# State-space output in the second block: rotated products added in pairs on GpSimd, two matrix terms per group on TensorE in place of four

## The chip, the core and the metric

The kernel runs on one core of a Trainium2 chip. The metric is the time of one execution on the device in microseconds (us), as a median over runs. The engines of the core are named here as in the profile: PE is TensorE (PEld its weight load), DVE is VectorE, ACT is ScalarE, POOL is GpSimd, and SP only issues transfers.

## What is computed

The program is two transformer-like blocks in a row, for 256 tokens of width 2048, in fp32. Each block projects, mixes (attention in the first; a matrix memory and a state-space layer in the second), and ends in an expert layer. The change is in the state-space layer of the second block: 64 heads ("groups" of the reference) of 16 inputs and 64 complex states each.

```
xr = einsum('bsgh,gph->bsgp', u, bbr);  xi = einsum('bsgh,gph->bsgp', u, bbi)
...
_, _, sr, si = lax.associative_scan(combine, (a_r, a_i, xr, xi), axis=1)
y = (einsum('bsgp,ghp->bsgh', sr, c_re) - einsum('bsgp,ghp->bsgh', si, c_im) + d * u)
ab = einsum('bsgh,ghk->bsgk', gelu(y), glu_w)
return ab[..., :16] * sigmoid(ab[..., 16:])
```

A state is multiplied at each token by a complex factor of size mag and angle th. The kernel turns the inputs by minus the angle of the token, so that two real scans with the factor mag remain, and turns the result back. With s0 and s1 for the two scanned states, cos and sin for the angle of the token, the output of a state pair is

```
sr = s0*cos - s1*sin        si = s0*sin + s1*cos
y  = c_re * (s0*cos - s1*sin) - c_im * (s0*sin + s1*cos) + d*u
```

## The kernel before

Weights are streamed. SP loads a tile of 128 output columns in two halves into `raw` (four buffers); ACT rounds each quarter to `w_hi` (L1427); DVE subtracts and writes the rest to `w_lo` (L1661, in `low`); PE multiplies each quarter three times (L1210 to L1212: high by high, high by low, low by high), 48 matmuls a tile. `w_hi` and `w_lo` hold one tile, so quarter c of the next tile can be prepared when PE has used quarter c of this one (`quarter_used`), and PE begins a quarter when `lo_ready` says so. A stage is a matrix; the one in question is `z2`, 41 tiles.

Other work is woven into a stage by hand, through generators that each engine advances once per tile. In `z2` that is the state-space layer: 32 groups g of two heads each (128 states on the partitions, 32 outputs), with j, i = divmod(g, 4). What each engine does for it, and in which place of its own row:

- PE, step k, ahead of tile k: `drive(k-2)` (L844, two matmuls, inputs to states) and `outputs(k-4)` (L857, four matmuls of 128x32 weights by 256 tokens), which waits for `ys_in`.
- DVE, step k: first `follow(k-3)`, which turns (L1022, L1023, with one operand in PSUM), adds (L1025, L1026) and scans (L1030, L1031, which raises `s_ready`). Then comes extra work that depends on i: `turns` for the next j at i = 0 (L1002 and L1003, eight small tensor_scalar), `near` at i = 1 (L1008 to L1010), `y_leave` at i = 2 (L992, reads PSUM); from step 20 a convolution in each step as well (L1042 and three L1044). After that the four L1661.
- POOL, group g: waits for `s_ready` and, from g = 2 on, until the outputs of group g-2 are done (`ys_done`), since `y_cos` and `y_sin` are double buffers; then L1602 and L1603, products of both scanned states with cos and with sin, 128x512 elements each. The second raises `ys_in`.
- ACT makes the tables of sin and cos once per j (L911, L912).

Group k-3 is thus turned back by POOL while DVE does the rest of its step k, and PE projects it in its step k+1, ahead of tile k+1.

The weights of the projection are blocks written by DVE beforehand, in `dve_s5_inputs`, whose steps lie between tiles of stage `v1` (experts of the first block): `c_blk` holds c_re, -c_re and -c_im. Instructions of one engine start in the order of the program; `link` makes DVE wait for its own last instruction.

Of the kernel before, what the change touches and what calls it, by code (L numbers as in the profile page):

```python
# [12 lines left out]
ALU = mybir.AluOpType  # L13
# [78 lines left out]
def build_two_blocks(nc, a):  # L92
# [3 lines left out]
    with ExitStack() as ctx:  # L96
# [3 lines left out]
        def sem(name):  # L100
            return ctx.enter_context(nc.semaphore(name))
# [26 lines left out]
        def flat(lo, hi):  # L128
            return work[:, lo:hi, :].rearrange("p r c -> p (r c)")
# [81 lines left out]
        c_raw = [flat(lo, lo + 2).rearrange("p (g h) -> p g h", h=16) for lo in (36, 38)]  # L211
# [1 line left out]
        b_tmp = flat(44, 46).rearrange("p (g h) -> p g h", h=16)  # L213
        b_blk = [flat(48, 52), flat(52, 56)]
        b_in = [flat(74, 78).rearrange("p (j s) -> p j s", s=P), flat(78, 82).rearrange("p (j s) -> p j s", s=P)]
        c_blk = [flat(82, 86), flat(86, 90), flat(90, 94)]
        cos_t = [rows(98, 102), rows(102, 106)]
        sin_t = [rows(106, 110), rows(110, 114)]
        turn_t, near_t = rows(114, 118), rows(118, 122)
# [1 line left out]
        x_rot, s_rot = rows(16, 18), rows(28, 32)  # L221
        y_cos, y_sin = rows(20, 24), rows(24, 28)
# [57 lines left out]
        blk_ready, bt_done, bt_out = sem("blk_ready"), sem("bt_done"), sem("bt_out")  # L280
        table_in, table_ready = sem("table_in"), sem("table_ready")
        xs_done, xs_used, s_ready = sem("xs_done"), sem("xs_used"), sem("s_ready")
        ys_in, ys_done, ys_out, y_gelu = sem("ys_in"), sem("ys_done"), sem("ys_out"), sem("y_gelu")
        glu_ready, glu_done, glu_sig, glu_out = sem("glu_ready"), sem("glu_done"), sem("glu_sig"), sem("glu_out")

# [547 lines left out]

        def pe_s5(pe):
            pe.wait_ge(bt_out, 4)
            pe.wait_ge(blk_ready, 5)

            def drive(g):
                j, i = divmod(g, 4)
                pe.wait_ge(tile_out, evac["z2"] + j + 1)  # L840
                if g >= 2:
                    pe.wait_ge(xs_used, g - 1)
                for part in range(2):
                    mm = pe.matmul(psum[:, 2 + g % 2, part * T:part * T + T], b_in[part][32 * i:32 * i + 32, j, :],  # L844
                                   z_u[32 * i:32 * i + 32, j, :], start=True, stop=True)
                mm.then_inc(xs_done, 1)

            def outputs(g):
                j, i = divmod(g, 4)
                pe.wait_ge(ys_in, g + 1)  # L850
                if i == 0 and j >= 2:
                    pe.wait_ge(ys_out, j - 1)
                out = psum[32 * i:32 * i + 32, 4 + j % 2, 0:T]
                b = 2 * (g % 2)
                terms = [(0, y_cos[:, b, :]), (1, y_sin[:, b + 1, :]), (2, y_sin[:, b, :]), (2, y_cos[:, b + 1, :])]
                for n, (m, rhs) in enumerate(terms):
                    mm = pe.matmul(out, c_blk[m][:, 32 * g:32 * g + 32], rhs, start=n == 0, stop=n == 3)  # L857
                mm.then_inc(ys_done, 1)

            for step in range(36):  # L860
                for g in in_step(step, 2, S5_TILES):
                    drive(g)
                for g in in_step(step, 4, S5_TILES):
                    outputs(g)
                yield
# [62 lines left out]
        def dve_s5_inputs(dve, link):  # L928
            L = lambda n: s5v[:, n, :]
            lre, lim, dt, mag, th, sin, cos = L(0), L(1), L(3), L(4), L(5), L(6), L(7)  # L930
            ar1, ai, d2, fr, fi, t0 = L(8), L(9), L(10), L(11), L(12), L(13)
            dve.wait_ge(s5_out, 1)
            dve.tensor_tensor(th, lim, dt, ALU.mult)
            dve.tensor_tensor(mag, lre, dt, ALU.mult).then_inc(s5_in, 1)
            dve.wait_ge(s5_in, 1)
            yield
            reduce_angle(dve, link, th, t0)
            link(dve.tensor_copy(sin, th))
            link(dve.scalar_tensor_tensor(cos, th, -1.0, th, ALU.mult, ALU.max))
            dve.tensor_scalar(cos, cos, -1.0, math.pi / 2, ALU.mult, ALU.add).then_inc(s5_in, 1)  # L940
            yield
            yield
            dve.wait_ge(s5_out, 3)
            link(dve.tensor_tensor(ar1, mag, cos, ALU.mult))
            dve.tensor_scalar(ar1, ar1, 1.0, None, ALU.subtract)
            dve.tensor_tensor(ai, mag, sin, ALU.mult)
            dve.tensor_tensor(d2, lre, lre, ALU.mult)
            link(dve.tensor_tensor(t0, lim, lim, ALU.mult))
            link(dve.tensor_tensor(d2, d2, t0, ALU.add))
            link(dve.reciprocal(d2, d2))  # L950
            for out, x, y, op in ((fr, ar1, ai, ALU.add), (fi, ai, ar1, ALU.subtract)):
                dve.tensor_tensor(out, x, lre, ALU.mult)
                link(dve.tensor_tensor(t0, y, lim, ALU.mult))
                link(dve.tensor_tensor(out, out, t0, op))
                link(dve.tensor_tensor(out, out, d2, ALU.mult))
            yield

            link(dve.tensor_scalar(th, th, 1 / (2 * math.pi), None, ALU.mult))
            g16 = [P, S5_TILES, 16]
            wide = lambda v: v.unsqueeze(2).broadcast_to(g16)  # L960
            for out, x, y, op in ((b_bar[0], b_raw[0], b_raw[1], ALU.subtract), (b_bar[1], b_raw[1], b_raw[0], ALU.add)):
                dve.tensor_tensor(out, x, wide(fr), ALU.mult)
                link(dve.tensor_tensor(b_tmp, y, wide(fi), ALU.mult))
                link(dve.tensor_tensor(out, out, b_tmp, op))
                yield
            blk4 = [P, S5_TILES, 2, 16]
            pair = c_pair.unsqueeze(1).unsqueeze(3).broadcast_to(blk4)

            def to_blocks(dst, src):
                dve.tensor_tensor(dst.rearrange("p (g q h) -> p g q h", q=2, h=16), src.unsqueeze(2).broadcast_to(blk4), pair,  # L970
                                  ALU.mult).then_inc(blk_ready, 1)

            to_blocks(b_blk[0], b_bar[0])
            yield
            to_blocks(b_blk[1], b_bar[1])
            yield
            to_blocks(c_blk[0], c_raw[0])
            yield
            dve.wait_ge(blk_ready, 3)
            link(dve.tensor_scalar(c_raw[0], c_raw[0], -1.0, None, ALU.mult))  # L980
            to_blocks(c_blk[1], c_raw[0])
            yield
            link(dve.tensor_scalar(c_raw[1], c_raw[1], -1.0, None, ALU.mult))
            to_blocks(c_blk[2], c_raw[1])
            yield

        def dve_s5(dve, link):
# [585 lines left out]
        @block.gpsimd  # L1573
        def _(pool):
            for blk in range(2):
                for k in range(16):
                    pool.wait_ge(tile_out, evac[f"out{blk + 1}"] + k + 1)
                    to = sq_one if k else sq_total
                    pool.tensor_tensor(to[:, 0, :], x1[:, k, :], x1[:, k, :], ALU.mult).then_inc(sq_tile, 1)
                    if k:  # L1580
                        pool.wait_ge(sq_tile, 31 * blk + 2 * k)
                        pool.tensor_tensor(sq_total[:, 0, :], sq_total[:, 0, :], sq_one[:, 0, :], ALU.add).then_inc(sq_tile, 1)
                        pool.wait_ge(sq_tile, 31 * blk + 2 * k + 1)
                pool.wait_ge(gate_out, GROUPS * (blk + 1))

                def weigh(i, slot):
                    pool.wait_ge(acts_loaded[slot], (i - slot) * 8 + (16 + 1024 * blk))
                    e = gate_e[:, i, :]
                    pool.tensor_tensor(e, acts_in[:, slot, :], e, ALU.mult).then_inc(weighed, 1)  # L1589

                tiles(pool, 0, 128, weigh)
                if blk == 0:

                    for g in range(S5_TILES):
                        j, i = divmod(g, 4)
                        cs, sn = (t[j % 2][:, i, :].unsqueeze(1).broadcast_to([P, 2, T]) for t in (cos_t, sin_t))
                        pool.wait_ge(s_ready, g + 1)

                        if g >= 2:
                            pool.wait_ge(ys_done, g - 1)  # L1600
                        b = 2 * (g % 2)
                        pool.tensor_tensor(y_cos[:, b:b + 2, :], s_rot[:, b:b + 2, :], cs, ALU.mult)  # L1602
                        pool.tensor_tensor(y_sin[:, b:b + 2, :], s_rot[:, b:b + 2, :], sn, ALU.mult).then_inc(ys_in, 1)  # L1603

# [374 lines left out]
```

## Time and profile before

| | us |
|---|---|
| median of 3 runs (lowest, highest) | 4474.46 (4473.86, 4475.19) |
| profiled execution, time | 4472.71 |
| profiled execution, span from first to last instruction | 4470.9 |
| PE busy / DVE busy / ACT busy / POOL busy | 4307.0 / 2988.2 / 2221.9 / 342.9 |
| stage z2 with the 32 groups, on the trace's own time | about 2304 to 2670 |
| share of PE, DVE in the chain that ended last | 87%, 10% |

A busy time says how long an engine had work in it, not that it was the one others waited for. Matmul records overlap: a record of 0.28 us with the next one 0.12 us later costs 0.12 us. For that reason costs are taken from start to start, both for PE and for DVE. A row of the time line is the start, the time from there to the end of the last of its instructions, engine, line, operation, tiles, shape and count, and in brackets how long the engine had been idle and who ended that. "issue" is idle time that no wait in the profile explains.

### The profile page before, as it was taken

What the parts mean: (1) busy time and instruction counts of PE and PEld (TensorE: products, weight loads), DVE (VectorE), ACT (ScalarE), POOL (GpSimd) and SP (SyncE); (2) the same over time, 40 slices, a digit from 0 to 9 for tenths busy, and PEclk for the clock granted to TensorE, in tenths of its full rate; (3) what the DMA queues carried; (4) which work ended last, traced back from release to release, by engine and by line L of the source; (5) the groups of instructions that cost most, each with busy time, mean ns of one, the idle gap of its engine ahead of it and who ended that gap; (6) DMA issues with size and microseconds to landing.
All of it is one profiled execution on the core that took longest, in us unless ns stands there. A gap on an engine that the chain in (4) does not pass through costs nothing.

```text
span 4470.9 us, 89367 instructions
## 1 busy us (share of the span) xinstructions
PE 4307.0 (96%) x29150; PEld 3965.4 (89%) x29150; DVE 2988.2 (67%) x5533; ACT 2221.9 (50%) x3910; POOL 342.9 (8%) x386
## 2 busy tenths in 40 slices
PE   7999999999999999999969897999999999999998
PEld 7989999999999988888857786999999998888887
DVE  5456677885666555565789976778766665556555
ACT  3345545775444455555523343466654444555554
POOL 0000010000000011111113210100000000111110
PEclk9999999999999999999989998999999999999999
DMA  6434555666555666766623332656655556667664
GB/s 212 148 95 142 179 183 190 207 205 193 177 178 177 192 217 217 235 217 225 206 97 114 97 121 94 203 175 205 206 184 177 177 179 200 217 217 234 217 216 160
DMA packets 276629, 814.36 MB, mean 182 GB/s; under 512 B 30768, under 2 KB 98096, under 8 KB 275248
## 3 DMA queue, kind: packets, MB, share of 16 engines
q1 hardware_dynamic: 273168, 804.38, 56.6%
q10 hardware_dynamic: 3360, 8.67, 0.5%
q8 instruction: 59, 0.97, 0.1%
q14 instruction: 42, 0.34, 0.0%
HBM read 770.98 MB, written 41.94 MB: 182 GB/s over the span
## 4 chain that ended last, share of the span: by engine, by line
PE 87%; DVE 10%; issue 1%; ACT 1%; DMA 1%; ACTq 0%; DVEq 0%; SPq 0%
PE psum L1210 17%; PE psum L1211 17%; PE psum L1212 17%; PE psum L387 10%; PE psum L389 10%; PE psum L388 10%; PE psum L370 3%; DVE sb_w_lo L1661 2%; PE psum L1296 1%; DVE sb_work L1044 1%; DVE sb_work L1031 0%; DVE sb_work L1626 0%; DVE sb_work L1023 0%; DVE sb_work L1022 0%; DVE sb_work L1642 0%
## 5 line engine op out<-in xcount | busy, mean ns | idle before, releaser
L1661 DVE TENSOR_TENSOR sb_w_lo<-sb_raw,sb_w_hi 128x512 fp32r<-128x512 f32 x2740 | 1892.8, 703 | 1329.9 <-ACT sb_w_hi L1427 1322.1
L1427 ACT CAST sb_w_hi<-sb_raw 128x512 fp32r<-128x512 f32 x2740 | 1695.7, 621 | 1983.4 <-PE psum L1212 1267.7
L1210 PE MATMUL psum<-sb_act_hl,sb_w_hi 128*128 128x256 f32 x6224 | 1789.2, 287 | 71.9 <-DVE sb_w_lo L1661 44.5
L1211 PE MATMUL psum<-sb_act_hl,sb_w_hi 128*128 128x256 f32 x6224 | 1769.1, 284 | 0.0
L1212 PE MATMUL psum<-sb_act_hl,sb_w_lo 128*128 128x256 f32 x6224 | 1768.6, 284 | 0.0
L1210 PEld LDWEIGHTS psum<-sb_act_hl,sb_w_hi 128*128 128x128 f32 x6224 | 1202.2, 193 | 93.5 <-issue 73.4
L1211 PEld LDWEIGHTS psum<-sb_act_hl,sb_w_hi 128*128 128x128 f32 x6224 | 1203.0, 193 | 0.7 <-issue 0.5
L1212 PEld LDWEIGHTS psum<-sb_act_hl,sb_w_lo 128*128 128x128 f32 x6224 | 1202.2, 193 | 0.0
L387 PE MATMUL psum<-sb_w_hi,sb_act_hl 128*128 128x512 f32 x2048 | 797.7, 390 | 6.1 <-DVE sb_w_lo L1661 6.1
L388 PE MATMUL psum<-sb_w_lo,sb_act_hl 128*128 128x512 f32 x2048 | 797.2, 389 | 0.0
L389 PE MATMUL psum<-sb_w_hi,sb_act_hl 128*128 128x512 f32 x2048 | 797.2, 389 | 0.0
L387 PEld LDWEIGHTS psum<-sb_w_hi,sb_act_hl 128*128 128x128 f32 x2048 | 384.8, 188 | 86.9 <-issue 6.1
L389 PEld LDWEIGHTS psum<-sb_w_hi,sb_act_hl 128*128 128x128 f32 x2048 | 384.7, 188 | 80.0
L388 PEld LDWEIGHTS psum<-sb_w_lo,sb_act_hl 128*128 128x128 f32 x2048 | 384.9, 188 | 79.7
L1589 POOL TENSOR_TENSOR sb_work<-sb_acts_in,sb_work 128x256 f32 x256 | 202.6, 792 | 2917.6 <-DMA sb_acts_in<-acts_mid 2917.6
L586 DVE TENSOR_SCALAR sb_scratch<-sb_consts,sb_slots 128x128 f32<-128x128 f32 x512 | 142.3, 342 | 0.0
L370 PE MATMUL psum<-sb_scratch 128*128 128x128 f32 x1024 | 134.6, 274 | 0.0
L594 DVE TENSOR_TENSOR sb_act_hl<-sb_work,sb_act_hl 128x256 fp32r<-128x256 f32 x256 | 117.8, 460 | 15.5 <-ACT sb_act_hl L455 15.4
L370 PEld LDWEIGHTS psum<-sb_scratch 128*128 128x128 f32 x1024 | 125.1, 191 | 0.0
L1210 PE MATMUL psum<-sb_x_hl,sb_w_hi 128*128 128x256 f32 x384 | 109.3, 285 | 1.1 <-DVE sb_w_lo L1661 1.1
L1211 PE MATMUL psum<-sb_x_hl,sb_w_hi 128*128 128x256 f32 x384 | 108.6, 283 | 0.0
L1212 PE MATMUL psum<-sb_x_hl,sb_w_lo 128*128 128x256 f32 x384 | 108.6, 283 | 0.0
(288 smaller groups left out, 2818.3 us busy)
## 6 DMA issues: line engine op xcount, KB each, us to landing
sb_raw<-in_u SPq DMA_DIRECT2D x512, 512.0 KB, 3.5
sb_raw<-in_v SPq DMA_DIRECT2D x512, 512.0 KB, 3.4
sb_raw<-in_w_z SPq DMA_DIRECT2D x82, 512.0 KB, 4.0
sb_raw<-in_w_gates SPq DMA_DIRECT2D x64, 512.0 KB, 3.5
sb_raw<-in_w_out SPq DMA_DIRECT2D x64, 512.0 KB, 3.4
acts_mid<-sb_acts_out SPq DMA_DIRECT2D x256, 128.0 KB, 3.4
sb_acts_in<-acts_mid SPq DMA_DIRECT2D x256, 128.0 KB, 3.2
sb_raw<-in_w_proj SPq DMA_DIRECT2D x56, 512.0 KB, 4.1
```

Of the source, the lines that this page charges most:

```text
L370: mm = pe.matmul(psum[:, 6 + half, j * P:j * P + P], onehot[:, 0, 4 * half + j, :], onehot[:, 1, 4 * half + j, :], start=True, stop=True)
L387: pe.matmul(ps, c_h, w_hi[:, c, :], start=first, stop=False, skip_group_check=True)
L388: pe.matmul(ps, c_h, w_lo[:, c, :], start=False, stop=False, skip_group_check=True)
L389: mm = pe.matmul(ps, c_l, w_hi[:, c, :], start=False, stop=False, skip_group_check=True)
L586: ins = dve.tensor_scalar(onehot[:, 1, 4 * half + j, :], iota, col, w, ALU.is_equal, ALU.mult)
L594: dve.tensor_tensor(act_hl[:, u, T:2 * T], gate_e[:, i, :], act_hl[:, u, 0:T].bitcast(F32), ALU.subtract).then_inc(c_lo, 1)
L1210: pe.matmul(ps, w_h, src[:, k, 0:T], start=start and kk == 0, stop=False)
L1211: pe.matmul(ps, w_h, src[:, k, T:2 * T], start=False, stop=False)
L1212: mm = pe.matmul(ps, w_l, src[:, k, 0:T], start=False, stop=stop and kk == 3)
L1427: act.copy(w_hi[:, c, :], raw[:, 2 * par + c // 2, (c % 2) * 512:(c % 2) * 512 + 512]).then_inc(hi_ready, 1)
L1589: pool.tensor_tensor(e, acts_in[:, slot, :], e, ALU.mult).then_inc(weighed, 1)
L1661: dve.tensor_tensor(w_lo[:, c, :], raw[:, 2 * par + c // 2, (c % 2) * 512:(c % 2) * 512 + 512], w_hi[:, c, :].bitcast(F32), ALU.subtract). ...
```

## The change

POOL gets two more instructions per group: it subtracts s1*sin from s0*cos in place, and adds s1*cos to s0*sin in place, each over 128x256. Both read what the two products wrote, so POOL waits ahead of them on a semaphore of its own, `ys_turned`. `ys_in` now comes from the last of the four. PE makes two matmuls per group, with c_re and with -c_im; the block -c_re is no longer built, and `dve_s5_inputs` has one step and two DVE instructions (L980, one L970) fewer.

```diff
-        c_blk = [flat(82, 86), flat(86, 90), flat(90, 94)]
+        c_blk = [flat(82, 86), flat(86, 90)]
...
+        ys_turned = sem("ys_turned")
...
-            pe.wait_ge(blk_ready, 5)
+            pe.wait_ge(blk_ready, 4)
...
-                terms = [(0, y_cos[:, b, :]), (1, y_sin[:, b + 1, :]), (2, y_sin[:, b, :]), (2, y_cos[:, b + 1, :])]
+                terms = [(0, y_cos[:, b, :]), (1, y_sin[:, b, :])]
                 for n, (m, rhs) in enumerate(terms):
-                    mm = pe.matmul(out, c_blk[m][:, 32 * g:32 * g + 32], rhs, start=n == 0, stop=n == 3)
+                    mm = pe.matmul(out, c_blk[m][:, 32 * g:32 * g + 32], rhs, start=n == 0, stop=n == 1)
...
             to_blocks(c_blk[0], c_raw[0])
             yield
-            dve.wait_ge(blk_ready, 3)
-            link(dve.tensor_scalar(c_raw[0], c_raw[0], -1.0, None, ALU.mult))
-            to_blocks(c_blk[1], c_raw[0])
-            yield
             link(dve.tensor_scalar(c_raw[1], c_raw[1], -1.0, None, ALU.mult))
-            to_blocks(c_blk[2], c_raw[1])
+            to_blocks(c_blk[1], c_raw[1])
             yield
...
                         pool.tensor_tensor(y_cos[:, b:b + 2, :], s_rot[:, b:b + 2, :], cs, ALU.mult)
-                        pool.tensor_tensor(y_sin[:, b:b + 2, :], s_rot[:, b:b + 2, :], sn, ALU.mult).then_inc(ys_in, 1)
+                        pool.tensor_tensor(y_sin[:, b:b + 2, :], s_rot[:, b:b + 2, :], sn, ALU.mult).then_inc(ys_turned, 1)
+                        pool.wait_ge(ys_turned, g + 1)
+                        pool.tensor_tensor(y_cos[:, b, :], y_cos[:, b, :], y_sin[:, b + 1, :], ALU.subtract)
+                        pool.tensor_tensor(y_sin[:, b, :], y_sin[:, b, :], y_cos[:, b + 1, :], ALU.add).then_inc(ys_in, 1)
```

POOL, at the end of its loop over the experts of stage v1 and at the first group of stage z2, before (L1589 is the loop's last multiplication, L1602 and L1603 are the two products):

```order
L1589 TENSOR_TENSOR sb_work<-sb_acts_in,sb_work 128x256
L307 REGISTER_ALU
L307 COMPARE_AND_BRANCH
L1602 TENSOR_TENSOR sb_work<-sb_work 128x512 [waits s_ready]
L1603 TENSOR_TENSOR sb_work<-sb_work 128x512
```

The same place after (lines have shifted; L1599 and L1600 are the products):

```order
L1586 TENSOR_TENSOR sb_work<-sb_acts_in,sb_work 128x256
L308 REGISTER_ALU
L308 COMPARE_AND_BRANCH
L1599 TENSOR_TENSOR sb_work<-sb_work 128x512 [waits s_ready]
L1600 TENSOR_TENSOR sb_work<-sb_work 128x512
L1602 TENSOR_TENSOR sb_work<-sb_work 128x256 [waits ys_turned]
L1603 TENSOR_TENSOR sb_work<-sb_work 128x256
```

Two instructions of half the size follow the products of each group, the first behind a wait.

PE, between the last matmul of one tile of z2 and the first of the next, before (L844 is `drive`, L857 is `outputs`):

```order
L1212 MATMUL psum<-sb_act_hl,sb_w_lo 128x256
L844 MATMUL psum<-sb_work 128x256 [waits xs_used,tile_out]
L844 MATMUL psum<-sb_work 128x256
L857 MATMUL psum<-sb_work 32x256 [waits ys_in]
L857 MATMUL psum<-sb_work 32x256 x3
L1210 MATMUL psum<-sb_act_hl,sb_w_hi 128x256 [waits lo_ready,tile_out]
```

After:

```order
L1209 MATMUL psum<-sb_act_hl,sb_w_lo 128x256
L845 MATMUL psum<-sb_work 128x256 [waits xs_used,tile_out]
L845 MATMUL psum<-sb_work 128x256
L858 MATMUL psum<-sb_work 32x256 [waits ys_in]
L858 MATMUL psum<-sb_work 32x256
L1207 MATMUL psum<-sb_act_hl,sb_w_hi 128x256 [waits lo_ready,tile_out]
```

Two matmuls of four are gone; the waits and the place are the same.

## Rows read from the trace of the kernel before

**Rows 1.** Stretches of z2: PE, PEld, DVE, ACT, POOL busy (count), clock, DMA.

```profile
2325.00:2400.00 75.00, 73.32 (x503) 60.66 (x502) 73.91 (x108) 27.18 (x46) 26.46 (x16) 1.00 0.38 119
2480.00:2560.00 80.00, 69.58 (x458) 58.36 (x459) 78.32 (x130) 23.25 (x40) 19.30 (x14) 0.96 0.33 103
```

**Rows 2.** Groups by line, 2317 to 2630: count, then busy us and mean ns, idle before.

```profile
L1210 PE MATMUL psum<-sb_act_hl,sb_w_hi 128*128 128x256 f32 x513 | 151.4, 295 | 25.1 <-DVE sb_w_lo L1661 25.1
...
L1661 DVE TENSOR_TENSOR sb_w_lo<-sb_raw,sb_w_hi 128x512 fp32r<-128x512 f32 x129 | 96.9, 811 | 0.3
...
L857 PE MATMUL psum<-sb_work 128*32 128x256 f32 x248 | 59.3, 382 | 0.0
```

**Rows 3.** Time line of one plain step (i = 3) on DVE and POOL.

```profile
2455.65 4.67 DVE L1661 TENSOR_TENSOR sb_w_lo<-sb_raw,sb_w_hi 128x512 fp32r<-128x512 f32 x4
2455.69 1.80 POOL L1602 TENSOR_TENSOR sb_work<-sb_work 128x512 f32<-128x512 f32 x1 [5.13 <-DVE sb_work L1031]
...
2457.45 1.71 POOL L1603 TENSOR_TENSOR sb_work<-sb_work 128x512 f32<-128x512 f32 x1
...
2460.24 0.68 DVE L1022 TENSOR_TENSOR sb_work<-psum,sb_work 128x512 f32<-128x512 f32 x1
```

**Rows 4.** The same step on PE.

```profile
2451.38 0.39 PE L1210 MATMUL psum<-sb_act_hl,sb_w_hi 128*128 128x256 f32 x1
...
2458.37 1.91 PE L857 MATMUL psum<-sb_work 128*32 128x256 f32 x8
2460.22 0.39 PE L1210 MATMUL psum<-sb_act_hl,sb_w_hi 128*128 128x256 f32 x1
```

**Rows 5.** DVE, the next step (i = 0, `turns`), with the four L1661 behind it.

```profile
2463.65 1.42 DVE L1002 TENSOR_SCALAR sb_work<-sb_consts,sb_work 128x128 f32<-128x128 f32 x1
...
2466.25 0.28 DVE L1002 TENSOR_SCALAR sb_work<-sb_consts,sb_work 128x128 f32<-128x128 f32 x1
...
2467.53 2.50 DVE L1661 TENSOR_TENSOR sb_w_lo<-sb_raw,sb_w_hi 128x512 fp32r<-128x512 f32 x4
2469.95 0.69 DVE L1022 TENSOR_TENSOR sb_work<-psum,sb_work 128x512 f32<-128x512 f32 x1
```

**Rows 6.** POOL in that step.

```profile
2463.69 1.29 POOL L1602 TENSOR_TENSOR sb_work<-sb_work 128x512 f32<-128x512 f32 x1 [4.53 <-DVE sb_work L1031]
2464.94 1.30 POOL L1603 TENSOR_TENSOR sb_work<-sb_work 128x512 f32<-128x512 f32 x1
```

**Rows 7.** DVE, `near` ahead of the first group (POOL idle) and in a later step.

```profile
2298.93 1.23 DVE L1009 SCALAR_TENSOR_TENSOR sb_work<-sb_work 128x1024 f32<-128x1024 f32 x1
...
2474.10 2.20 DVE L1009 SCALAR_TENSOR_TENSOR sb_work<-sb_work 128x1024 f32<-128x1024 f32 x1
```

**Rows 8.** DVE, the convolution beside POOL's products, and with POOL idle.

```profile
2495.77 1.50 DVE L1042 TENSOR_SCALAR sb_work<-sb_work,sb_cols 128x256 f32<-128x256 f32 x1
2497.30 2.41 DVE L1044 SCALAR_TENSOR_TENSOR sb_work<-sb_work,sb_cols 128x255 f32<-128x255 f32 x3
...
2552.84 0.35 DVE L1042 TENSOR_SCALAR sb_work<-sb_work,sb_cols 128x256 f32<-128x256 f32 x1
2553.23 1.52 DVE L1044 SCALAR_TENSOR_TENSOR sb_work<-sb_work,sb_cols 128x255 f32<-128x255 f32 x3
```

**Rows 9.** POOL in stage out1: a square, and an addition in place behind a wait.

```profile
607.31 0.61 POOL L1579 TENSOR_TENSOR sb_work<-sb_work 128x256 f32<-128x256 f32 x1 [5.04 <-DVE sb_work L1845]
608.00 0.74 POOL L1582 TENSOR_TENSOR sb_work<-sb_work 128x256 f32<-128x256 f32 x1
```

**Rows 10.** The longest wait of PE between two tiles, and the stretch behind it.

```profile
2568.16 0.55 PE L1210 MATMUL psum<-sb_act_hl,sb_w_hi 128*128 128x256 f32 x1 [3.79 <-DVE sb_w_lo L1661]
...
2570.00:2575.00 5.00, 5.00 (x28) 5.00 (x28) 4.86 (x9) 1.23 (x2) 1.79 (x2) 0.57 0.57 197
```

**Rows 11.** Stage v1 beside `dve_s5_inputs`, and z2 after the last group.

```profile
2160.00:2170.00 10.00, 10.00 (x46) 8.29 (x45) 8.27 (x13) 5.38 (x10) 1.48 (x2) 1.00 0.68 218
...
2650.00:2655.00 5.00, 5.00 (x44) 5.00 (x43) 2.39 (x4) 2.99 (x5) 0.00 (x0) 1.00 0.79 263
```

## Prediction, made before the changed kernel ran

> **What bounds the kernel now.** The change touches stage z2 alone, so I read that stage and nothing else of the 4471 us. First the busy times by stretch [rows 1]: POOL is busy 26 us of 75 in the first half, PE 73.3, and DVE 73.9 of 75 and 78.3 of 80. Two engines look full, so a busy share does not decide it. Then the groups by line with the idle time before them [rows 2]: between 2317 and 2630 PE waited 25.1 us for the `w_lo` that DVE writes (L1661), while DVE waited 0.3 us in front of its 129 L1661. DVE waits for nobody, PE waits for DVE: in these 313 us DVE sets the pace. The time line of one step shows it too. Four L1661 start at 2455.65 and the next group's L1022 starts at 2460.24, right behind them [rows 3], although PE had done everything that L1022 needs.
>
> The same rows show why DVE is so full. Four L1661 take 2467.53 to 2469.95, 2.42 us, when POOL is idle [rows 5], and 4.59 us when POOL's two products run beside them [rows 3]. So 2.17 us of DVE's time per step is lost to POOL's work. It is the same in every kind of step:
> - `turns`: from 2463.65 to 2466.25 DVE does two instructions that are worth 0.28 us each at most, 0.19 from start to start [rows 5]; the first seems to end with L1602, the second with L1603 [rows 6]. Lost: 2.60 - 0.38 = 2.2.
> - `near`: L1009 takes 2.20 beside POOL and 1.23 alone [rows 7], and L1010 behind it does the same. Lost: about 1.9.
> - convolution: L1042 and three L1044 take 1.50 + 2.41 beside POOL, 0.35 + 1.52 alone [rows 8]. Lost: 2.04.
>
> The mean of the four is 2.1 us of DVE for two products which alone take 1.29 + 1.30 = 2.59 us of POOL [rows 6]. That is 0.81 us of DVE for each microsecond of POOL's work. (Where DVE's instruction shares the time, POOL is slowed too, to 1.80 and 1.71 [rows 3]; I count its time as it is alone.)
>
> **The change, part by part.**
>
> *PE loses two matmuls per group.* The four L857 of a group are 8 records and last from 2458.37 to 2460.22, 1.85 us [rows 4]; half is 0.92 us, times 32 groups 29.5 us of PE. Almost all of it is in front of a tile whose `w_lo` comes from DVE, so it turns into a longer wait of PE. PE needs 8.84 us per step without waiting, from L1210 at 2451.38 to L1210 at 2460.22 [rows 4]; DVE takes 9.4 in the first half (75 us with 16 instructions of POOL, so 8 groups [rows 1]). What is worth something is the last group: behind it PE runs without a gap, 5.00 of 5 us, and DVE is idle half the time [rows 11]. I take -0.9 us, one group.
>
> *POOL gains a subtraction and an addition per group*, 128x256 each. No row shows them in this place. From above they cost POOL 0.74 us each, the addition in place of stage out1, which had a DVE instruction beside it; from below 0.61, the square in the same stage [rows 9]. Half of a product is 1.29 / 2 = 0.65 [rows 6], and I take that, since it reads two different tensors and is free of DVE. So 1.30 us of POOL per group, times 0.81: 1.05 us of DVE. What DVE does at that time decides whether it counts. The products end 3.5 us behind the scan in a plain step, when over 1 us of L1661 is still to come (4.59 - 3.50 [rows 3]); in `turns`, `near` and convolution steps there is more, since the four L1661 come behind them. So the new work lies beside DVE's instructions with SBUF operands in every kind of step. DVE has no idle time to give [rows 2]. Times 32 groups: +33.7 us.
>
> *The wait on `ys_turned`* holds only POOL, for its own product. The addition in out1 started 0.08 us behind the end of the square [rows 9], with such a wait. Behind POOL's row stands PE's `outputs` one step later: POOL's end moves from 3.5 to some 5.4 us behind the scan, PE asks for it in the next step of over 9 us, behind a tile of 5.8. It does not wait. The next products of POOL are asked for 8 to 10 us apart. Cost 0; if it did delay PE, PE has the 0.92 us and its earlier wait to give.
>
> *DVE loses L980 and one L970 in stage v1.* PE is busy 10.00 of 10 us there and DVE 8.3 [rows 11], so nothing comes of it, and later work of v1 moving up by a tile changes nothing either. Cost 0 in both directions.
>
> **Sum.** 4470.9 + 33.7 - 0.9 = 4503.7 us of span. The median of the runs shown lies 3.6 us above the span of the profiled execution (4474.46 against 4470.9, of which 1.8 is around the span in that execution): 4507.3, I say 4507.
>
> Bounds of the POOL term: low, 0.61 us each and the 0.74 us of DVE per microsecond of POOL that `near` shows (1.9 / 2.59): 32 x 1.22 x 0.74 = 29. High, 0.74 us each and all of it lost to DVE: 32 x 1.48 = 47. That is 4499 to 4521, the other terms as they are.
>
> The Trainium skill has the loss as a rule: GPSIMD Engine Reference, Key points, says that GpSimd shares its SBUF interfaces with VectorE and contends with DVE instructions in a 2-port mode or with two SBUF inputs. The rows on L1661, L1009, L1044 (two SBUF inputs) and L1002 (one, blocked till POOL ends) agree. By the same sentence L1022 and L1023, which have one operand in PSUM, would not be held up, which no row here shows. The same page, Instruction dispatch, puts a two-input body at about 2.5 cycles per element at a 1.2 GHz clock; by that the new instructions would be an estimated 0.53 us each and the sum 32 x 1.06 x 0.81 = 27 us in place of 33.7. The products would be 1.07 us by it and are 1.29 to 1.30 in the rows, so I keep the rows.
>
> **Rivals.**
>
> *PE sets the pace, the kernel gets faster.* PE is busier than any other engine over the run and nearly full here. If its 0.92 us per group came off the end, the time would be 4474.5 - 29.5 = 4445. For it to happen DVE would have to wait for PE. The rows speak against it, with 0.3 us of such waiting in 313 [rows 2]. Chance 0.05.
>
> *The new work hides.* If it fell beside L1022, L1023 and the other instructions with a PSUM operand, some 1.2 us per step, and these lost nothing by it, DVE would pay little. It decides by place: the new work would have to begin more than 4.6 us behind the scan in a plain step, and it begins at 3.6 [rows 3]. Or POOL's shorter instructions may find gaps that the long ones did not. The price is then 0 to 8 us, 4474 to 4482. Chance 0.07.
>
> *PE becomes the bound by its clock, on the slower side.* PE's waits grow from 0.8 us per step (25.1 us [rows 2] over 31) to 2.8 (0.92 less work, 1.05 longer steps). Behind a wait of 3.79 us the granted clock was 0.57 over the next 5 us, and PE made 28 matmuls where it makes 44 in a full stretch [rows 10, 11]: between the two levels of 1.2 and 2.4 GHz, mostly at the lower. That is (44 - 28) / 44 x 5 = 1.8 us of PE's work lost in these 5, and I take twice that, 3.6, as the most. A step of DVE would then be 9.4 + 1.05 = 10.4 us and one of PE 8.84 - 0.92 + 3.6 = 11.5, so PE would be late by 1.1 us; it decides from a loss of 2.5 us per step. Once in each of 31 steps it would be +34 us; a step in which PE is late has no idle time ahead of it, so at most every other step, +17: 4524. The DVE row beside the clock of 0.57 is still full, 4.86 of 5 [rows 10], so in this kernel such a fall costs nothing yet. Chance 0.1.
>
> **Chances and range.** Forecast (4499 to 4521) 0.78, clock 0.1 (4515 to 4524), hidden 0.07, faster 0.05. The range takes in the bounds of the POOL term and a part of the two neighbours: 4493 to 4522. About 0.2% (9 us) is what a measurement of this kernel can tell from no change. Faster by more: 0.05. Within: 0.08. Slower by more: 0.87.
>
> **What would show it.** In the profile after: four L1661 of a plain step at about 5.7 us in place of 4.59; DVE still without idle time between the first and the last group; that stretch about 33 us longer; the two new POOL lines at 0.65 to 0.9 us each (slowed like the products); PE's wait for L1661 grown from 25 us to about 85; PE's clock a little lower in the stage, with no wait of DVE for PE. Wrong would be: DVE idle in front of L1661 with ACT or PE as the releaser (then PE had become the bound), L1022 and L1023 longer than 0.68 (then instructions with a PSUM operand lose as well), or the L1661 at 4.6 as before (then the new work costs DVE nothing).

## The result, and the profile after

| | median us (lowest, highest) | span of the profiled execution |
|---|---|---|
| before | 4474.16 (4472.22, 4475.19) | 4470.9 |
| changed | 4500.57 (4498.31, 4502.79) | 4496.5 |

The changed kernel takes 1.006 times as long, with a 95% interval of 1.0042 to 1.0077: 26.4 us slower. The profiled executions differ by 25.6 us.

Nearly all of it lies in the 32 groups of stage z2. L1602 of the first group starts at 2317.03 in the kernel before and L1599, the same product, at 2317.45 in the changed one; that of the last group starts at 2621.61 and at 2647.49. So the 31 intervals between them take 304.58 us before and 330.04 after, 25.5 us more, or 0.82 us per group.

The groups by line of the changed kernel between 2317 and 2660, in the form of [rows 2]; lines have shifted, L1207 is the first matmul of a tile, L858 the projection, L1602 and L1603 are POOL's new instructions:

```profile
L1207 PE MATMUL psum<-sb_act_hl,sb_w_hi 128*128 128x256 f32 x520 | 163.1, 314 | 57.8 <-DVE sb_w_lo L1661 57.8
...
L1661 DVE TENSOR_TENSOR sb_w_lo<-sb_raw,sb_w_hi 128x512 fp32r<-128x512 f32 x132 | 109.0, 883 | 1.7 <-ACT sb_w_hi L1424 1.3
...
L858 PE MATMUL psum<-sb_work 128*32 128x256 f32 x128 | 33.6, 385 | 0.0
L1602 POOL TENSOR_TENSOR sb_work<-sb_work 128x256 f32<-128x256 f32 x32 | 33.0, 1031 | 2.5
L1603 POOL TENSOR_TENSOR sb_work<-sb_work 128x256 f32<-128x256 f32 x32 | 30.6, 955 | 0.0
```

PE's projection is about halved (33.6 us busy where it was 59.3), and PE waits more: 57.8 us for DVE's L1661 in place of 25.1. An L1661 takes 883 ns in the mean where it took 811 [rows 2]. DVE still waits for nobody in front of its L1661, 1.7 us in 343.

DVE has the same instructions as before, and they take longer. Its groups by line between the first and the last group's product, before (2317 to 2621):

```profile
L1661 DVE TENSOR_TENSOR sb_w_lo<-sb_raw,sb_w_hi 128x512 fp32r<-128x512 f32 x124 | 93.7, 816 | 0.3
L1044 DVE SCALAR_TENSOR_TENSOR sb_work<-sb_work,sb_cols 128x255 f32<-128x255 f32 (+2 forms) x42 | 28.3, 675 | 1.5
L1002 DVE TENSOR_SCALAR sb_work<-sb_consts,sb_work 128x128 f32<-128x128 f32 x28 | 15.7, 560 | 0.2
```

The same after (2317 to 2647; L1041 and L999 are the lines that were L1044 and L1002):

```profile
L1661 DVE TENSOR_TENSOR sb_w_lo<-sb_raw,sb_w_hi 128x512 fp32r<-128x512 f32 x124 | 103.9, 896 | 0.4
L1041 DVE SCALAR_TENSOR_TENSOR sb_work<-sb_work,sb_cols 128x255 f32<-128x255 f32 (+2 forms) x42 | 35.6, 848 | 1.5
L999 DVE TENSOR_SCALAR sb_work<-sb_consts,sb_work 128x128 f32<-128x128 f32 x28 | 19.0, 679 | 0.2
```

These three are busy 10.2, 7.3 and 3.3 us longer. L1000 (L1003 before) adds 3.2 us and L1039 (L1042 before) 1.4. Together that is 25.4 us, all of the 25.5 that the stage lost.

The stretches of [rows 1], in the changed kernel. DVE is as full as it was (73.91 and 78.32 us then), PE has lost 5.6 and 7.4 us of busy time, and its granted clock is 0.92 and 0.85 in place of 1.00 and 0.96:

```profile
2325.00:2400.00 75.00, 67.72 (x439) 58.32 (x438) 73.97 (x94) 26.23 (x44) 42.14 (x30) 0.92 0.35 112
2480.00:2560.00 80.00, 62.19 (x384) 55.08 (x384) 78.43 (x118) 22.57 (x37) 32.07 (x28) 0.85 0.29 92
```

A plain step (i = 3), DVE and POOL, to be read beside [rows 3]:

```profile
2469.41 5.22 DVE L1661 TENSOR_TENSOR sb_w_lo<-sb_raw,sb_w_hi 128x512 fp32r<-128x512 f32 x4
2474.56 0.68 DVE L1019 TENSOR_TENSOR sb_work<-psum,sb_work 128x512 f32<-128x512 f32 x1
...
2469.46 1.78 POOL L1599 TENSOR_TENSOR sb_work<-sb_work 128x512 f32<-128x512 f32 x1 [3.93 <-DVE sb_work L1028]
2471.19 1.75 POOL L1600 TENSOR_TENSOR sb_work<-sb_work 128x512 f32<-128x512 f32 x1
2473.02 1.07 POOL L1602 TENSOR_TENSOR sb_work<-sb_work 128x256 f32<-128x256 f32 x1
2474.05 1.19 POOL L1603 TENSOR_TENSOR sb_work<-sb_work 128x256 f32<-128x256 f32 x1
```

The four L1661 take 5.15 us from start to start, 0.56 more than before. POOL works until 2475.24, and its last 0.7 us lie beside L1019, which reads one operand from PSUM and takes 0.68 us as always.

A `turns` step, to be read beside [rows 5, 6]. The first L999 shown here slips in between POOL's second product and the subtraction; the two instructions behind it each end just after one of POOL's:

```profile
2480.50 0.27 DVE L999 TENSOR_SCALAR sb_work<-sb_consts,sb_work 128x128 f32<-128x128 f32 x1
2480.70 0.74 DVE L1000 TENSOR_SCALAR sb_work<-sb_consts,sb_work 128x128 f32<-128x128 f32 x1
2481.36 0.76 DVE L999 TENSOR_SCALAR sb_work<-sb_consts,sb_work 128x128 f32<-128x128 f32 x1
2482.04 0.27 DVE L1000 TENSOR_SCALAR sb_work<-sb_consts,sb_work 128x128 f32<-128x128 f32 x1
...
2480.58 0.78 POOL L1602 TENSOR_TENSOR sb_work<-sb_work 128x256 f32<-128x256 f32 x1
2481.32 0.72 POOL L1603 TENSOR_TENSOR sb_work<-sb_work 128x256 f32<-128x256 f32 x1
```

And the four L1661 behind `near`, beside the end of POOL's L1602 and its L1603:

```profile
2453.35 3.55 DVE L1661 TENSOR_TENSOR sb_w_lo<-sb_raw,sb_w_hi 128x512 fp32r<-128x512 f32 x4
2456.82 0.68 DVE L1019 TENSOR_TENSOR sb_work<-psum,sb_work 128x512 f32<-128x512 f32 x1
...
2452.43 1.59 POOL L1602 TENSOR_TENSOR sb_work<-sb_work 128x256 f32<-128x256 f32 x1
2453.97 1.18 POOL L1603 TENSOR_TENSOR sb_work<-sb_work 128x256 f32<-128x256 f32 x1
```

They take 3.47 us, where four with POOL idle took 2.42 [rows 5]: 1.05 more.

### The profile page after: what moved, and what is told of

Same layout as the page of the kernel before. It is cut to its first block, busy times and chain, and to the rows that moved or that the text cites. A ratio compares the mean times of both kernels' runs of the same rounds, so it can differ in the third digit from the quotient of the medians.

```text
span 4496.5 us, 89187 instructions
## 1 busy us (share of the span) xinstructions
PE 4301.4 (96%) x29022; PEld 3973.3 (88%) x29022; DVE 3002.7 (67%) x5531; ACT 2222.0 (49%) x3910; POOL 408.2 (9%) x450
## 4 chain that ended last, share of the span: by engine, by line
PE 87%; DVE 10%; issue 1%; ACT 1%; DMA 1%; ACTq 0%; SPq 0%; DVEq 0%
PE psum L1207 17%; PE psum L1208 17%; PE psum L1209 17%; PE psum L388 10%; PE psum L389 10%; PE psum L390 10%; DVE sb_w_lo L1661 3%; PE psum L371 3%; DVE sb_work L1041 1%; PE psum L1293 1%; DVE sb_work L1028 0%; DVE sb_work L1626 0%; DVE sb_work L1020 0%; DVE sb_work L1642 0%; DVE sb_work L1019 0%
## 5 line engine op out<-in xcount | busy, mean ns | idle before, releaser
L1661 DVE TENSOR_TENSOR sb_w_lo<-sb_raw,sb_w_hi 128x512 fp32r<-128x512 f32 x2740 | 1893.7, 703 | 1342.2 <-ACT sb_w_hi L1424 1335.2
L1207 PE MATMUL psum<-sb_act_hl,sb_w_hi 128*128 128x256 f32 x6224 | 1799.5, 289 | 104.0 <-DVE sb_w_lo L1661 77.1
L1207 PEld LDWEIGHTS psum<-sb_act_hl,sb_w_hi 128*128 128x128 f32 x6224 | 1212.7, 195 | 125.8 <-issue 105.4
L1207 PE MATMUL psum<-sb_x_hl,sb_w_hi 128*128 128x256 f32 x384 | 109.3, 285 | 0.5 <-DVE sb_w_lo L1661 0.5
```

What stands on the lines that cost most here:

```text
L1207: pe.matmul(ps, w_h, src[:, k, 0:T], start=start and kk == 0, stop=False)
L1661: dve.tensor_tensor(w_lo[:, c, :], raw[:, 2 * par + c // 2, (c % 2) * 512:(c % 2) * 512 + 512], w_hi[:, c, :].bitcast(F32), ALU.subtract). ...
```

## The experiments

**My theory** was that DVE sets the pace of these steps, that POOL's additions cost time because they slow DVE's instructions, and that PE's saving ends in its waits. **The rivals:** PE's saving was gained and POOL's cost is twice as large; the loss is PE's lower clock; the loss is the longer way from scan to projection.

In the table, "31 intervals" is the time from the product of the first group to that of the last, as above. A round is four groups, from POOL's first product in a `near` step to that in the next; the table has the fourth round of the stage and the fifth, and from the fifth on each step has a convolution.

| kernel | POOL additions | matmuls per group | median us | 31 intervals | round 4 | round 5 |
|---|---|---|---|---|---|---|
| before | 0 | 4 | 4474.2 | 304.6 | 36.69 | 43.59 |
| changed | 2 | 2 | 4500.6 | 330.0 | 40.28 | 46.74 |
| e1_adds_four | 2 | 4 | 4497.9 | 329.8 | 40.22 | 46.72 |
| e2_no_adds_two | 0 | 2 | 4471.5 | 305.0 | 36.92 | 43.59 |
| e3_adds_aside | 2, off the path | 4 | 4499.2 | 329.9 | 40.27 | 46.69 |
| e4_adds_twice | 4 | 2 | 4525.0 | 355.5 | 42.88 | 50.52 |
| e7_adds_on_dve | 0 (2 on DVE) | 2 | 4495.8 | 325.2 | 39.29 | 46.24 |
| e5_before_early | 0 | 4 | 4452.2 | 280.7 | 35.36 | 39.08 |
| e6_after_early | 2 | 2 | 4467.4 | 296.9 | 36.06 | 42.31 |
| e8_early_two | 0 | 2 | 4436.1 | 268.9 | 32.05 | 39.05 |

The kernel before ran at 4473.55 beside e1 to e4 and at 4473.38 beside e5 to e8.

### e1_adds_four: the additions with four matmuls

```diff
-                terms = [(0, y_cos[:, b, :]), (1, y_sin[:, b, :])]
+                terms = 2 * [(0, y_cos[:, b, :]), (1, y_sin[:, b, :])]
...
-                    mm = pe.matmul(out, c_blk[m][:, 32 * g:32 * g + 32], rhs, start=n == 0, stop=n == 1)
+                    mm = pe.matmul(out, c_blk[m][:, 32 * g:32 * g + 32], rhs, start=n % 2 == 0, stop=n % 2 == 1)
```

> The changed kernel with four matmuls per group again on PE (the two terms are projected twice, the second pair starts the sum anew), POOL's two additions kept. Theory (DVE sets the pace of the stage, PE's share lies in its waits): the time of the changed kernel, 4500.6, plus at most 0.9 for the last group, 4500 to 4503. Rival 1 (both engines count, PE's saving of 29.5 us was gained and POOL's additions cost 56): 4530. Rival 2 (the loss comes from PE's lower clock in its longer waits): PE waits less, its clock in the stage rises from 0.89 towards 0.97, and the time falls below 4495.

Measured: 4497.91 (4496.06 to 4501.23), ratio to before 1.0058 (1.0041 to 1.0074), 2 us under the 4500 that I had given as the least. Giving PE its 29 us of work back changes nothing: the 31 intervals are 329.8 us against 330.0. The stretch from 2317 to 2640 of the changed kernel and of e1, in the columns of [rows 1]:

```profile
2317.00:2640.00 323.00, 270.85 (x1707) 235.09 (x1705) 317.68 (x439) 99.28 (x168) 154.37 (x123) 0.88 0.31 98
```

```profile
2317.00:2640.00 323.00, 281.53 (x1826) 233.66 (x1825) 317.72 (x440) 99.44 (x168) 153.92 (x123) 0.95 0.30 98
```

PE is busier by 10.7 us and its clock goes from 0.88 to 0.95, while DVE's busy time is the same to 0.04 us. So the lower clock of the changed kernel is real and costs nothing here: it is paid out of PE's waits. That rival and the one of the doubled price fall.

### e2_no_adds_two: two matmuls, no additions

Two of the four terms are left out.

```diff
-                terms = [(0, y_cos[:, b, :]), (1, y_sin[:, b + 1, :]), (2, y_sin[:, b, :]), (2, y_cos[:, b + 1, :])]
+                terms = [(0, y_cos[:, b, :]), (2, y_sin[:, b, :])]
...
-                    mm = pe.matmul(out, c_blk[m][:, 32 * g:32 * g + 32], rhs, start=n == 0, stop=n == 3)
+                    mm = pe.matmul(out, c_blk[m][:, 32 * g:32 * g + 32], rhs, start=n == 0, stop=n == 1)
```

> The kernel before with two of its four matmuls per group left out (c_re by the first, -c_im by the second product of the first scanned state only) and no additions on POOL; two terms of the output are not computed. Theory: DVE's work is unchanged, so the time is that of before less the last group's 0.9: 4473 to 4474. Rival 1 (PE's saving counts): 4445. Rival 2 (more idle time lowers PE's clock and that costs time): slower than before, above 4480.

Measured: 4471.51 (4469.06 to 4475.84), ratio 0.9996 (0.9987 to 1.0006), a little under the 4473 to 4474 expected and not to be told from the kernel before. The half of the change that was to bring something brings nothing that can be measured. What PE saved, it waits and does more slowly: its granted clock between the first and the last group is 0.90 in place of 0.97. e1 and e2 together are the change taken apart. In the 31 intervals the additions alone cost 25.2 us, and the two matmuls fewer bring nothing (+0.4).

### e3_adds_aside: the additions off the path to the projection

```diff
+        y_spare = rows(18, 20)
...
                         pool.tensor_tensor(y_sin[:, b:b + 2, :], s_rot[:, b:b + 2, :], sn, ALU.mult).then_inc(ys_in, 1)
+                        pool.wait_ge(ys_in, g + 1)
+                        pool.tensor_tensor(y_spare[:, 0, :], y_cos[:, b, :], y_sin[:, b + 1, :], ALU.subtract)
+                        pool.tensor_tensor(y_spare[:, 1, :], y_sin[:, b, :], y_cos[:, b + 1, :], ALU.add).then_inc(ys_turned, 1)
```

PE projects the products with four matmuls, as before. (POOL also waits on `ys_turned` ahead of the next group, and DVE once ahead of the gated unit, so that nothing is overwritten.)

> The kernel before with its four matmuls, which still read the products as soon as they are there; POOL makes the two additions behind that and writes them to a place that nobody reads, so they delay no wait of PE. Theory (the additions cost DVE time through the SBUF operands of both): as slow as the changed kernel, 4499 to 4504. Rival (the time comes from the longer way from scan to projection: one more wait and 1.6 us more before PE may project): 4474, as before.

Measured: 4499.24 (4498.33 to 4503.21), ratio 1.0059 (1.0042 to 1.0076). No wait of PE depends on these additions, and they cost all that the change costs. The longer way to the projection is not it.

### e4_adds_twice: twice the additions

```diff
+        y_spare = rows(18, 20)
...
+                        pool.tensor_tensor(y_spare[:, 0, :], y_cos[:, b, :], y_sin[:, b + 1, :], ALU.subtract)
+                        pool.tensor_tensor(y_spare[:, 1, :], y_sin[:, b, :], y_cos[:, b + 1, :], ALU.add)
                         pool.tensor_tensor(y_cos[:, b, :], y_cos[:, b, :], y_sin[:, b + 1, :], ALU.subtract)
```

> The changed kernel with POOL's subtraction and addition made twice per group, the first time into a place that nobody reads. Theory: a further 1.5 us of POOL per group. If DVE always paid the same for it, 0.8 us per group as in the change, 4526. In plain steps part of it now falls beside L1019 and L1020, with an operand in PSUM, and is free there: I expect 4515 to 4526. Rival (only the longer way to the projection counts, and from some point PE is held up by it): each of the 32 groups costs the 1.5 us in full, 4549.

Measured: 4524.99 (4521.18 to 4525.48), ratio 1.0115 (1.0098 to 1.0132). The second pair costs as much as the first, 25.5 us in the 31 intervals. I had expected somewhat less, because a plain step would let part of it pass for free. It does, a `y_leave` step does so wholly, and the steps with a convolution cost more. A plain step, DVE and POOL (L1664 writes `w_lo`, L1020 and L1021 turn the inputs, L1023 and L1024 add, the lines of the second pair are L1605 and L1606):

```profile
2480.66 5.22 DVE L1664 TENSOR_TENSOR sb_w_lo<-sb_raw,sb_w_hi 128x512 fp32r<-128x512 f32 x4
2485.81 0.68 DVE L1020 TENSOR_TENSOR sb_work<-psum,sb_work 128x512 f32<-128x512 f32 x1
2486.41 0.67 DVE L1021 TENSOR_TENSOR sb_work<-psum,sb_work 128x512 f32<-128x512 f32 x1
2487.11 0.42 DVE L1023 TENSOR_TENSOR sb_work<-sb_work 128x256 f32<-128x256 f32 x1
2487.46 0.96 DVE L1024 TENSOR_TENSOR sb_work<-sb_work 128x256 f32<-128x256 f32 x1
...
2485.30 1.19 POOL L1604 TENSOR_TENSOR sb_work<-sb_work 128x256 f32<-128x256 f32 x1
2486.44 0.74 POOL L1605 TENSOR_TENSOR sb_work<-sb_work 128x256 f32<-128x256 f32 x1
2487.14 0.99 POOL L1606 TENSOR_TENSOR sb_work<-sb_work 128x256 f32<-128x256 f32 x1
```

The four L1664 take 5.15 us again, L1020 and L1021 are untouched beside L1604 and L1605. Of the instructions with two operands in SBUF behind them, L1023 starts just ahead of L1606 and is untouched too, and L1024 pays: 0.96 us in place of 0.42. So a plain step pays 0.54 us for the second pair. In a `y_leave` step the second pair lies almost wholly beside L1020 and L1021, and the step takes 9.17 us with one pair and 9.18 with two. A step with a convolution and nothing else pays more for the second pair than for the first: 9.67 us before, 10.36 in the changed kernel, 11.41 here. Round 4 grows by 2.60 us and round 5 by 3.78, where the first pair cost 3.59 and 3.15. The equal sums, 25.5 us each time, are thus a coincidence of unequal steps.

### e7_adds_on_dve: the additions on DVE

```diff
+            def turn_back(g):
+                b = 2 * (g % 2)
+                dve.wait_ge(ys_turned, g + 1)
+                dve.tensor_tensor(y_cos[:, b, :], y_cos[:, b, :], y_sin[:, b + 1, :], ALU.subtract)
+                dve.tensor_tensor(y_sin[:, b, :], y_sin[:, b, :], y_cos[:, b + 1, :], ALU.add).then_inc(ys_in, 1)
...
+                    for g in in_step(step, 4, S5_TILES):
+                        turn_back(g)
                     for g in in_step(step, 3, S5_TILES):
...
-                        pool.wait_ge(ys_turned, g + 1)
-                        pool.tensor_tensor(y_cos[:, b, :], y_cos[:, b, :], y_sin[:, b + 1, :], ALU.subtract)
-                        pool.tensor_tensor(y_sin[:, b, :], y_sin[:, b, :], y_cos[:, b + 1, :], ALU.add).then_inc(ys_in, 1)
```

> The changed kernel with the subtraction and the addition of a group made by DVE at the start of its next step, in place of POOL; PE has two matmuls. Theory: DVE pays for them itself, 0.34 us from start to start each by L1022's neighbours of the same shape (L1025, L1026), about 0.7 us per group with no POOL work beside, against 0.86 us that it lost to POOL's additions: 32 x 0.7 = 22, 4494 to 4498, no slower than the changed kernel. Rival (GpSimd's additions were in truth mostly hidden, and the loss comes from elsewhere, the extra wait or the clock): putting them on the full engine adds its time on top, 4520 and more.

Measured: 4495.75 (4494.79 to 4496.58), ratio 1.0052 (1.0035 to 1.0069). The start of a step on DVE, with the two additions (L1035, L1036) in front of L1019:

```profile
2444.18 0.42 DVE L1035 TENSOR_TENSOR sb_work<-sb_work 128x256 f32<-128x256 f32 x1
2444.52 0.42 DVE L1036 TENSOR_TENSOR sb_work<-sb_work 128x256 f32<-128x256 f32 x1
2444.86 0.69 DVE L1019 TENSOR_TENSOR sb_work<-psum,sb_work 128x512 f32<-128x512 f32 x1
```

They take 0.68 us of DVE, and the 31 intervals are 20.6 us longer than before, 0.66 per group. The same work on POOL took 0.82 us of DVE. Giving these additions away to GpSimd cost VectorE more than doing them.

### e5_before_early: POOL's products beside instructions with a PSUM operand

Work is neither added nor left out. DVE turns the next group's inputs right behind this group's scans, and PE drives one step earlier.

```diff
-                for g in in_step(step, 2, S5_TILES):
+                for g in in_step(step, 1, S5_TILES):
                     drive(g)
...
-            def follow(g):
+            def turn_in(g):
...
                 dve.tensor_tensor(x_cos, x, cs, ALU.mult)
                 dve.tensor_tensor(x_sin, x, sn, ALU.mult).then_inc(xs_used, 1)
+
+            def follow(g):
+                m = mag[:, g:g + 1].broadcast_to([P, T])
                 dve.wait_ge(xs_used, g + 1)
...
+                        if g == 0:
+                            turn_in(0)
                         follow(g)
+                        if g + 1 < S5_TILES:
+                            turn_in(g + 1)
```

> The kernel before with one thing moved: DVE turns the inputs of the next group (L1022, L1023, one operand in PSUM each) right behind the scans of this group, at the time when POOL makes its products; PE's drive comes a step earlier for it. No work is added or left out. Theory (POOL takes time from DVE only while DVE reads two SBUF operands or runs a one-operand instruction in SBUF; an operand in PSUM leaves POOL alone): 1.2 us of POOL's 2.6 per group is now beside instructions that lose nothing, which gives DVE about 1 us per step; PE with its 8.84 us per step then becomes the bound in the first half (9.2 before) and DVE stays it in the second (10.9 to 9.9): 4452 to 4462. Rival (POOL slows every DVE instruction that touches SBUF, whatever else it reads): L1022 and L1023 become longer, and the time is that of before, 4474.

Measured: 4452.15 (4449.54 to 4454.74), ratio 0.9956 (0.994 to 0.9973). It beats both kernels. A plain step, DVE and POOL (L1021 and L1022 are the turning, L1668 writes `w_lo`):

```profile
2449.74 0.69 DVE L1021 TENSOR_TENSOR sb_work<-psum,sb_work 128x512 f32<-128x512 f32 x1
2450.35 0.68 DVE L1022 TENSOR_TENSOR sb_work<-psum,sb_work 128x512 f32<-128x512 f32 x1
2451.62 1.26 DVE L1668 TENSOR_TENSOR sb_w_lo<-sb_raw,sb_w_hi 128x512 fp32r<-128x512 f32 x1 [0.59 <-ACT sb_w_hi L1434]
...
2449.79 1.30 POOL L1609 TENSOR_TENSOR sb_work<-sb_work 128x512 f32<-128x512 f32 x1 [5.31 <-DVE sb_work L1034]
2451.04 1.29 POOL L1610 TENSOR_TENSOR sb_work<-sb_work 128x512 f32<-128x512 f32 x1
```

L1021 and L1022 last 0.69 and 0.68 us beside POOL's first product, and that product 1.30 us as when it is alone, where in [rows 3] both slowed each other. DVE now waits in front of this L1668 for ACT, which waits for PE. The waits of e5 between the first group's product and the last one's, 2319 to 2600 (us in total, times, the longest):

```profile
DVE sb_w_lo L1668 <- ACT sb_w_hi L1434: 10.6, 18, 0.8
...
PE psum L1217 <- DVE sb_w_lo L1668: 6.8, 4, 2.7
```

All of DVE's 10.6 us lie ahead of 2480, in the first half. The stretch 2325 to 2400 in the columns of [rows 1] has PE without a gap and DVE with one:

```profile
2325.00:2400.00 75.00, 75.00 (x509) 62.42 (x509) 69.46 (x112) 27.37 (x46) 24.84 (x18) 0.98 0.39 127
```

Round 4 takes 35.36 us, four times the 8.84 us that PE needs without waiting [rows 4]. PE bounds the first half of this version. In the second DVE still sets the pace, and there the whole gain shows: a step with a convolution and nothing else takes 8.44 us in place of 9.67, 1.2 us less, about as long as L1021 and L1022 together.

### e8_early_two: the same with two matmuls

The edits of e5 and of e2 together; two terms are left out.

> The kernel with the early turning, without additions, and with two of the four matmuls of each group left out (two terms of the output are not computed). It shows whether PE bounds the early version: then its 0.92 us per group counts now. Theory: the first half goes from PE's 8.84 to DVE's 8.2 us a step, the second stays with DVE: 8 to 14 us faster than the early version with four matmuls. Rival (DVE bounds that version too): the same time as that one, within 2 us.

Measured: 4436.09 (4435.39 to 4437.11), ratio 0.9919 (0.9902 to 0.9935), 16 us faster than e5, a little more than I had expected. Round 4 falls from 35.36 to 32.05 us, 0.83 a step of the 0.92 that PE saves, and round 5 stays, 39.08 and 39.05. The same edit of PE is worth nothing in e2 and 16 us here. It does not compute the output; it shows where PE's saving counts.

### e6_after_early: the changed kernel with the same move

The edit of e5, made in the changed kernel.

> The changed kernel with the same move of L1019 and L1020 (the turning of the next group's inputs) to right behind the scans. Theory: as above, about 1 us per step back in turns, near and convolution steps; in plain steps less, since there a part of the additions already fell beside them: 4500.6 less 25 to 30, 4470 to 4476. PE has 7.9 us of work a step and does not bound. Rival (every DVE instruction is slowed): 4500.

Measured: 4467.4 (4466.49 to 4471.93), ratio 0.999 (0.998 to 1.0). 33 us less than the changed kernel, where 25 to 30 were expected, and 15 more than e5. POOL's work beside L1018 and L1019 is free here too; what comes behind it is not. So even in the better order the change (additions for matmuls) loses: 296.9 us against 280.7 in the 31 intervals.

## Why the prediction was right, and what was mis-sized

The time fell in the range (4493 to 4522) and below the forecast: +26.4 us where +33 was said. The mechanism was right; the term of POOL's additions was too large, and the 25.5 us measured for it lie below its own lower bound of 29. The lower bound of the time, 4499, was also reckoned wrongly: it leaves out the 3.6 us between span and median that the upper one (4521) has in it. With them it is 4502.6, above the 4500.57 measured. That the range held is owed in part to its margin down to 4493. Point by point:

- **DVE sets the pace, PE's 29.5 us end in its waits.** Right. e2 gives 0 for the matmuls alone, e1 gives them back at no cost. PE's wait for L1661 grew to 57.8 us, not to the 85 forecast, for two reasons. DVE's loss was 8 us smaller than forecast. And PE worked more slowly at the lower clock: a record of L1207 is 314 ns in place of 295, and PE's busy time between the first and the last group fell only from 281.3 us to 276.1, though 29.5 us of work had been taken away.
- **The last group's 0.9 us.** From the last group's first product to the end of the span it is 1849.29 us before and 1849.01 after, 0.3 less. Too large a term, of no weight.
- **POOL's new instructions, 0.65 us each.** Too low. Beside the short DVE instructions of `turns` they take 0.78 and 0.72, 1.50 us for the pair, and beside L1021 with its PSUM operand (e4) 0.74. That is the 0.74 of the addition in out1, which I had taken as the upper bound and put down to a DVE instruction beside it. In the mean over all steps, where DVE slows them, they take 1.03 and 0.96, above the 0.65 to 0.9 that I had named as the sign in the profile. The Trainium skill's 2.5 cycles per element (GPSIMD Engine Reference, Instruction dispatch), an estimated 0.53 us, lay further off still. The difference between a product (1.25 us from start to start) and an addition (0.72) is 0.53 us, so the rows agree with it for the added elements and show some 0.2 us on top that do not grow with the size (an estimate from these two rows, of different operations).
- **0.81 us of DVE per microsecond of POOL.** Too high for this work, and this is the term that put the sum off. 0.82 us per group for 1.50 us of POOL is 0.55. The mean over the old products was used for work that comes behind them, and the kinds of step differ. Plain: 0.56 us, since DVE's four L1661 are through after 5.15 us (I had said 5.7) and the rest of POOL's work lies beside L1019, with its PSUM operand. `turns`: one DVE instruction slips into POOL's gap and the next two are held, so that the stretch from the first L999 to the first L1661 takes 4.77 us in place of 3.88, 0.9 more. `near`: 1.05, as forecast. `y_leave`: 1.1, its four L1661 taking 5.37 us in place of 4.28. A convolution and nothing else: 0.7 (9.67 to 10.36). Two errors, 1.30 for 1.50 and 0.81 for 0.55, partly made up for each other.
- **The wait on `ys_turned` costs nothing.** Right: from the end of L1600 (2472.94) to the start of L1602 it is 0.08 us, PE waited 0.7 us in all for L1603, and e3, where PE does not wait for the additions, is as slow.
- **Stage v1.** Right: the first group's product starts at 2317.45 in place of 2317.03, and in e2, which has all of the old steps in v1, at 2319.87, so it moves by more than that from run to run.
- **The rival "PE becomes the bound by its clock".** The clock fell as it said, to 0.88 over the stage, and DVE's time did not move by it (e1, with 0.95). PE has the room. It has less than I had reckoned: a step in the first half took DVE 9.17 us before (a quarter of round 4), not 9.4, against PE's 8.84.
- **The rival "hidden".** Both of its mechanisms are there in part. In plain steps the end of POOL's work lies beside L1019, which took about half of the forecast's loss (0.56 us in place of 1.05). In `turns` steps an L999 finds a gap. I had given hiding a chance of 0.07 as a whole and nothing as a share of the term.

The rule that GpSimd contends with DVE instructions in a 2-port mode or with two SBUF inputs (Trainium skill, GPSIMD Engine Reference, Key points) was in the prediction with the remark that no row showed its other half. e5 agrees: with one operand in PSUM, 0.69 and 0.68 us beside POOL, and the product at its 1.30 us.

## What to carry to other kernels

Find the engine that waits for nobody in the stage before giving another one less to do: two matmuls fewer per group were worth 0 us as long as VectorE set the pace, and 16 us when it no longer did. GpSimd is no free helper for a full VectorE. In the mean over the steps a microsecond of its products took 0.81 us from VectorE here, and a microsecond of its additions, part of which fell beside instructions that lose nothing, 0.55. For the additions that was more than VectorE needed to make them itself (0.82 us against 0.68 per group); for the products no run tried it. Work for GpSimd goes beside VectorE instructions that read PSUM; that move alone gave 21 us.

## What the runs showed of the hardware beyond that

In `turns` steps an addition or subtraction on GpSimd of two different tensors of 128x256 took 0.72 to 0.78 us, and a product of 128x512 in one instruction 1.25 to 1.30. Two instructions of half the size thus took 1.50 us and a gap of 0.08. No run halves one and the same operation, so what halving costs is not shown, only that these two small ones were not as cheap as one large one.

Between the first and the last group PE's longest wait for L1661 was 3.8 us before (15 waits) and 4.9 in the changed kernel (21 waits). Such a wait of 4.86 us ended at 2483.58; the granted clock was 0.55 in the stretch 2480 to 2485, 0.76 in the next 5 us and 1.00 in the 5 after those: down from TensorE's level of 2.4 GHz towards that of 1.2, and back. Over the stretch 2317 to 2630 it was 0.97 before, 0.88 after and 0.86 with the additions made twice. e1, at 0.95 with the same time as the changed kernel, shows that this cost nothing here: TensorE had waits to pay from.
